# Transposing the feed-forward activations on VectorE and with small DMAs in place of TensorE, in a two-layer decoder trunk

## What is computed

```python
def swiglu(x, w_gate, w_up, w_down):
    return (jax.nn.silu(x @ w_gate) * (x @ w_up)) @ w_down

for layer in range(DEPTH):
    h = h + 0.5 * swiglu(rms_norm(h, ln_ffn1[layer]), ffn1_w_gate[layer], ffn1_w_up[layer], ffn1_w_down[layer])
    u = rms_norm(h, ln_mix[layer])
    ...
    h = h + 0.5 * swiglu(rms_norm(h, ln_ffn2[layer]), ffn2_w_gate[layer], ffn2_w_up[layer], ffn2_w_down[layer])
return rms_norm(h, final_norm)
```

## Time and profile before

| | us |
|---|---|
| median of 3 runs | 977.7 |
| lowest and highest | 976.63, 978.82 |
| span of the profiled execution, first to last instruction | 974.3 |
| TensorE busy | 954.1 |
| VectorE busy | 522.1 |
| ScalarE busy | 456.0 |
| GpSimd busy | 99.3 |

### The profile page before, as it was taken

The page is one execution under the profiler, slowest core; times in us unless marked ns, Lnnn a source line. Parts: engine busy times, 40 slices in busy tenths (PEclk is TensorE's granted clock), DMA queues, the critical chain, the costliest instruction groups (busy, mean ns, idle before and its releaser), DMA issues.

```text
span 974.3 us, 11825 instructions
## 1 busy us (share of the span) xinstructions
PE 954.1 (98%) x4572; PEld 789.0 (81%) x4572; DVE 522.1 (54%) x480; ACT 456.0 (47%) x583; POOL 99.3 (10%) x170
## 2 busy tenths in 40 slices
PE   6999999999999999999999999999998999999997
PEld 5888888888877888888888888888886888888885
DVE  3654454463576655554466555544547465555442
ACT  4554452354676544443344444433456454444431
POOL 3800000025311100000003000000023010000000
PEclk9999999999999999999999999999999999999999
DMA  9866655444522556664564566645544056665421
GB/s 273 275 199 194 215 196 216 173 173 173 194 89 85 173 178 197 198 226 171 177 201 140 186 200 197 246 163 197 192 151 131 3 185 200 196 199 227 152 113 44
DMA packets 121211, 172.92 MB, mean 177 GB/s; under 512 B 5456, under 2 KB 97632, under 8 KB 121168
## 3 DMA queue, kind: packets, MB, share of 16 engines
q1 hardware_dynamic: 120848, 171.99, 51.9%
q0 software_dynamic: 320, 0.34, 0.4%
HBM read 171.25 MB, written 1.05 MB: 177 GB/s over the span
## 4 chain that ended last, share of the span: by engine, by line
PE 92%; DVE 3%; ACT 2%; DMA 1%; SPq 1%; issue 0%; DVEq 0%; POOLq 0%; POOL 0%; ACTq 0%
PE bank L392 57%; PE bank L427 19%; PE bank L431 9%; PE bank L445 4%; DMA raw<-in_ffn_w_up 1%; DVE w_lo L1353 1%; ACT h L1154 1%; DVE mx L1454 1%; PE bank L612 1%; PE bank L547 1%; ACT w_hi L1051 1%; PE bank L570 1%; SPq L775 1%; ACT silu L1154 0%; DVE shared L1479 0%; PE bank L408 0%
## 5 line engine op out<-in xcount | busy, mean ns | idle before, releaser
L1353 DVE TENSOR_TENSOR w_lo<-raw,w_hi 128x2048 fp32r<-128x2048 f32 x152 | 348.6, 2295 | 224.6 <-ACT w_hi L1051 224.6
L1051 ACT ACTIVATE w_hi<-raw 128x2048 fp32r<-128x2048 f32 x152 | 291.7, 1920 | 204.9 <-PE bank L392 115.1
L392 PE MATMUL bank<-w_hi,xT_hi 128*128 128x512 f32 x832 | 331.2, 398 | 5.3 <-DVE w_lo L1535 5.3
L392 PE MATMUL bank<-w_hi,xT_lo 128*128 128x512 f32 x832 | 325.7, 392 | 0.0
L392 PE MATMUL bank<-w_lo,xT_hi 128*128 128x512 f32 x832 | 325.3, 391 | 0.0
L392 PEld LDWEIGHTS bank<-w_hi,xT_hi 128*128 128x128 f32 x832 | 157.0, 189 | 37.6 <-issue 3.6
L392 PEld LDWEIGHTS bank<-w_hi,xT_lo 128*128 128x128 f32 x832 | 156.9, 189 | 33.6
L392 PEld LDWEIGHTS bank<-w_lo,xT_hi 128*128 128x128 f32 x832 | 157.3, 189 | 30.9
L427 PE MATMUL bank<-w_hi,hT_hi 128*128 128x512 f32 x348 | 136.6, 392 | 0.0
L427 PE MATMUL bank<-w_lo,hT_hi 128*128 128x512 f32 x348 | 135.5, 389 | 0.0
L431 PE MATMUL bank<-w_hi,hT_lo 128*128 128x512 f32 x348 | 107.3, 389 | 0.0
(11 more groups left out here) (142 smaller groups left out, 627.3 us busy)
## 6 DMA issues: line engine op xcount, KB each, us to landing
raw<-in_ffn_w_gate SPq DMA_DIRECT2D x88, 512.0 KB, 4.2
raw<-in_ffn_w_up SPq DMA_DIRECT2D x88, 512.0 KB, 5.3
raw<-in_ffn_w_down SPq DMA_DIRECT2D x88, 512.0 KB, 4.2
raw<-in_a_w_qkv SPq DMA_DIRECT2D x24, 512.0 KB, 5.0
raw<-in_a_w_o SPq DMA_DIRECT2D x8, 512.0 KB, 4.0
raw<-in_b_w_q SPq DMA_DIRECT2D x8, 512.0 KB, 4.8
raw<-in_b_w_o SPq DMA_DIRECT2D x8, 512.0 KB, 3.9
vec<-in_ln_ffn SPq DMA_DIRECT2D x4, 512.0 KB, 5.7
```

What stands on the lines that cost most here:

```text
L392: mm = nc.tensor.matmul(bank[b][:, :], xs[:, kt, own(pos)], ws[:, slot(u), cols], start=(kt == 0 and i == 0), stop=(kt == KT - 1 and i == 2))
L1051: nc.scalar.activation(w_parts(u)[0], raw[:, slot(u), :], ACT.Copy).then_inc(s_hi, 1)
L1353: nc.vector.tensor_tensor(lo, raw[:, slot(u), :], hi.bitcast(F32), ALU.subtract).then_inc(s_lo, 1)
```

## The change

The transposes of the five full blocks leave TensorE. VectorE transposes the block of 128x512 in squares of 32x32 into the buffer of `silu` (called `turned`), with the column groups reordered. SyncE then issues 16 DMAs from SBUF to SBUF, each 32 partitions x 128 columns (16 KB), which put square row a, column group q to partition group q, columns of a, in the first 512 columns of `xn` (called `landed`). ScalarE and VectorE read `landed` for hi and lo in place of a PSUM bank. The last 256 columns are still transposed by TensorE. The moves of pos 0 stand in SyncE's queue eight ahead of a unit's load and eight ahead of the next one's; those of pos 1 are together behind a turn's loads. On ScalarE and VectorE the parts of pos 0 move behind silu/mul(1,1), those of pos 1 into the next turn, behind its first two splits, and those of block 4 of pos 1 ahead of silu/mul(1,0) at the end of the stage. The down stage waits for a count of the lo parts in place of PSUM reads. SyncE's `gate_up`, the vectors and the `rows` of a feed-forward are joined in one `ffn`; the order of the loads among themselves stays.

```diff
+        turned = [silu[:, pos, :, :].rearrange("p j n -> p (j n)") for pos in range(NPOS)]
+        landed = [xn[:, pos, 0:BANK] for pos in range(NPOS)]
...
+        def block_no(f, g):
+            return H_BLOCKS * f + g + 1
...
-        FILLED_PER_TURN = 4
+        FILLED_PER_TURN = 2
...
# TensorE
                     gate_up(4 * g, 1, 0, g, turn)
-                    h_transposes(0, (f, g), turn)
                     gate_up(4 * g + 2, 1, 1, g, turn)
                     gate_up(4 * g + 4, 0, 0, g + 1, turn)
-                    h_transposes(1, (f, g), turn)
...
-                h_transposes(0, (f, 5), n_tiles=2)
+                h_transposes(0, f)
...
-                pe.wait_ge(s_read[4], uses[4] - 1)
+                pe.wait_ge(s_hT_lo[0], block_no(f, H_BLOCKS - 1))
                 down((0, 1), 0)
-                h_transposes(1, (f, 5), n_tiles=2)
+                h_transposes(1, f)
                 down((2,), 0)
-                pe.wait_ge(s_read[6], uses[6] - 1)
+                pe.wait_ge(s_hT_lo[1], block_no(f, H_BLOCKS - 1))
...
# SyncE
+            def h_move(f, pos, g, rows):
+                sp.wait_ge(s_turned[pos], block_no(f, g))
+                for a in rows:
+                    for q in range(4):
+                        sp.dma_start(landed[pos][32 * q:32 * (q + 1), P * a:P * (a + 1)],
+                                     turned[pos][32 * a:32 * (a + 1), P * q:P * (q + 1)]).then_inc(s_hT[pos], 16)
...
+                with sp.Fori(0, LOOP_TURNS) as turn:
+                    for k in range(2):
+                        h_move(f, 0, turn, (2 * k, 2 * k + 1))
+                        unit(u0 + 8 + k, k, turn * (2 * CH) + 4 * CH, turn)
+                    for k in range(2):
+                        unit(u0 + 10 + k, k, turn * (2 * CH) + 5 * CH, turn)
+                    h_move(f, 1, turn, range(4))
                 for k in range(2):
+                    h_move(f, 0, 3, (2 * k, 2 * k + 1))
                     unit(u0 + 20 + k, k, CH * (N_CHUNK - 1))
+                for name in vectors:
+                    vector(name)
+                down(0, 1)
+                h_move(f, 1, 3, range(4))
+                for k in range(2):
+                    h_move(f, 0, 4, (2 * k, 2 * k + 1))
+                    down(2 + k)
+                down(4, 5)
+                h_move(f, 1, 4, range(4))
+                down(*range(6, DN_UNITS))
...
# ScalarE
+                def h_hi(pos, g, turn=0):
+                    act.wait_ge(s_hT[pos], (block_no(f, g) + turn) * 16 * H_MOVES)
+                    nc.scalar.activation(hT_hi[:, bass.ds((g + turn) * 4, 4), own(pos)].rearrange("p t (q s) -> p t q s", q=4),
+                                         landed[pos].rearrange("p (q t s) -> p t q s", q=4, t=4),
+                                         ACT.Copy).then_inc(s_hipart, 1)
...
                     split(u0 + 4 * g + 4, turn)
                     split(u0 + 4 * g + 5, turn)
+                    if g:
+                        h_hi(1, g - 1, 0 if turn is None else turn)
                     silu_gate(1, 0, g, turn)
-                    h_hi(0, g, turn)
                     split(u0 + 4 * g + 6, turn)
                     split(u0 + 4 * g + 7, turn)
                     silu_gate(1, 1, g, turn)
+                    h_hi(0, g, 0 if turn is None else turn)
                     silu_gate(0, 0, g + 1, turn)
-                    h_hi(1, g, turn)
...
                 split(u0 + 24)
                 split(u0 + 25)
+                h_hi(1, 4)
                 silu_gate(1, 0, 5)
...
# VectorE
+                def h_turned(pos, g, turn=0):
+                    b, n = taken["gu", f, g, 1, pos]
+                    dve.wait_ge(s_read[b], n + turn)
+                    nc.vector.transpose(turned[pos].rearrange("p (q t s) -> p t q s", q=4, t=4),
+                                        h[:, pos, :].rearrange("p (t q s) -> p t q s", t=4, q=4)
+                                        ).then_inc(s_turned[pos], 1)
...
+                    h_turned(0, g, 0 if turn is None else turn)
                     split(u0 + 4 * g + 4, turn)
                     split(u0 + 4 * g + 5, turn)
+                    if g:
+                        h_lo(1, g - 1, 0 if turn is None else turn)
                     mul(1, 0)
-                    h_lo(0, g, turn)
                     split(u0 + 4 * g + 6, turn)
                     split(u0 + 4 * g + 7, turn)
                     mul(1, 1)
+                    h_turned(1, g, 0 if turn is None else turn)
+                    h_lo(0, g, 0 if turn is None else turn)
                     mul(0, 0)
-                    h_lo(1, g, turn)
```

More of the change, by code:

```diff
@@ L53 @@
 FFN_UNITS = GU_UNITS + DN_UNITS
+H_BLOCKS = N_CHUNK // 2
+H_MOVES = 16
 HEADS = 8
@@ L238, in trunk @@
         s_silu = sem("s_silu")
+        s_turned = [sem(f"s_turned{i}") for i in range(NPOS)]
+        s_hT = [sem(f"s_hT{i}") for i in range(NPOS)]
+        s_hT_lo = [sem(f"s_hT_lo{i}") for i in range(NPOS)]
         s_hipart = sem("s_hipart")
@@ L460, in x_ready, with h_transposes @@
                     in_sbuf(pe, ("xT", name, pos, j))
[L462 to L467, removed]
+            def h_transposes(pos, f):
+                b = acc(pos, 0)
+                pe.wait_ge(s_read[b], uses[b])
+                transposes([h[:, pos, P * i:P * (i + 1)] for i in range(2)], 4 + 2 * pos, ("hT", f, pos))
             def ffn(f, u0, name, next_name):
@@ L785, in unit @@
                              for i, w in enumerate((gate, up))], turn)
-                for k in range(4):
+                for k in range(8):
                     unit(u0 + k, k % 2, CH * (k // 2))
@@ L790, in gate_up, with down @@
                         load_x(1)
-                with sp.Fori(0, 4) as turn:
-                    for k in range(4):
-                        unit(u0 + 4 + k, k % 2, turn * (2 * CH) + CH * (2 + k // 2), turn)
+                def down(*ts):
+                    view = w_down[l].rearrange("(k p) n -> p k n", p=P)
+                    for i in ts:
+                        u = u0 + GU_UNITS + i
+                        dst = raw[:, slot(u), :].rearrange("p (k n) -> p k n", k=2)
+                        load(u, [(dst[:, k, :], view[:, 2 * i + k, :]) for k in range(2)])
+                with sp.Fori(0, LOOP_TURNS) as turn:
[5 more added lines that the diff above has]
+                    h_move(f, 1, turn, range(4))
                 for k in range(2):
+                    h_move(f, 0, 3, (2 * k, 2 * k + 1))
                     unit(u0 + 20 + k, k, CH * (N_CHUNK - 1))
+                for name in vectors:
[8 more added lines that the diff above has]
+                down(*range(6, DN_UNITS))
             def rows(u0, n, w):
@@ L836, in _ @@
             vector("ln_ffn1_0")
[L837 to L841, removed]
+            ffn(0, U_FFN1_0, a["ffn1_w_gate"], a["ffn1_w_up"], a["ffn1_w_down"], 0, "ln_mix_0", "ln_ffn2_0", "kv_norm")
             columns(U_QKV, 6, a["a_w_qkv"][0])
@@ L844, in _ @@
             vector("ln_ffn1_1")
-            gate_up(U_FFN2_0, a["ffn2_w_gate"], a["ffn2_w_up"], 0)
-            vector("ln_mix_1")
-            rows(U_FFN2_0 + GU_UNITS, DN_UNITS, a["ffn2_w_down"][0])
+            ffn(1, U_FFN2_0, a["ffn2_w_gate"], a["ffn2_w_up"], a["ffn2_w_down"], 0, "ln_mix_1")
             dst = raw[:, slot(U_KV), :].rearrange("p (k g c) -> p k g c", k=KT, g=2)
@@ L850, in _ @@
                         for i, w in enumerate(("kv_w_k", "kv_w_v"))])
[L851 to L854, removed]
+            ffn(2, U_FFN1_1, a["ffn1_w_gate"], a["ffn1_w_up"], a["ffn1_w_down"], 1, "b_b_q", "b_b_o")
             columns(U_WQ, 2, a["b_w_q"][0])
@@ L857, in _ @@
             vector("ln_ffn2_1")
-            gate_up(U_FFN2_1, a["ffn2_w_gate"], a["ffn2_w_up"], 1)
-            vector("final_norm")
-            rows(U_FFN2_1 + GU_UNITS, DN_UNITS, a["ffn2_w_down"][1])
+            ffn(3, U_FFN2_1, a["ffn2_w_gate"], a["ffn2_w_up"], a["ffn2_w_down"], 1, "final_norm")
             sp.wait_ge(s_xn, xn_count("final_norm", 0))
@@ L1091, in silu_gate, with h_last_hi @@
                     nc.scalar.activation(silu[:, pos, j, :], bank[acc(pos, j)][:, 0:CH], ACT.Silu).then_inc(s_silu, 1)
[L1093 to L1096, removed]
+                def h_hi(pos, g, turn=0):
[3 more added lines that the diff above has]
+                                         ACT.Copy).then_inc(s_hipart, 1)
+                def h_last_hi(pos):
+                    hi_part(hT_hi[:, FT - 2:FT, own(pos)], 4 + 2 * pos, ("hT", f, pos), 2)
                 def turn_of(g, turn=None):
@@ L1122, in ffn @@
                 split(u0 + 25)
+                h_hi(1, 4)
                 silu_gate(1, 0, 5)
-                h_hi(0, 5, n_tiles=2)
-                h_hi(1, 5, n_tiles=2)
+                h_last_hi(0)
+                h_last_hi(1)
                 for i in range(26, 33):
@@ L1407, in mul, with h_lo, h_last_lo @@
                                             ALU.mult).then_inc(s_read[b], 1)
```

(16 more changed lines are left out.)

2 lines of the change are left out of this document (1 added, 1 removed).

## The result

The change makes the kernel slower: 1063.67 us median (4 runs, 1061.92 to 1064.24) beside 977.96 for the kernel before on the same chip, a ratio of 1.0877 with a 95% interval of 1.0862 to 1.0892. The forecast was 959.3 us. The profiled span is 1062.2 us where it was 974.3. (In every execution that has both on record the time is 1.8 us above the span. So 974.3 stands for some 976.1 us, a little low for the kernel before, and the 3.4 us between its span and its median are partly chance.)

The account below looks back on a forecast made before the run. TensorE, busy 954.1 of 974.3 us, was taken as the bound; removing 40 transpose groups at 0.46 saves 18.4, added work costs zero, giving a 955.9 span plus 3.4, 959.3 us; range 957 to 966.

Parts of the forecast that it names:

- The saving: Gate/up stage on TensorE: 40 groups of four transposes removed at 0.46 us each, 18.4 us off the path.
- added durations: Rival reading of TensorE's transposes: durations add up, 160 x 0.272 = 43.5 us saved, 934.2 us; chance of its rival 0.01.
- VectorE and ScalarE's order: Feed-forward: VectorE's 40 added transposes at 0.69 us fit idle time, ScalarE stays ready for its next silu; cost zero.
- the price of an issue: SyncE's queue: each small move taken at 0.34 us, between almost nothing and 0.77; no stall under 0.48.
- The second term of the same sum: SyncE's queue in a full turn: four load pairs at 0.80 us beside 32 moves, 14.1 us in all.
- The upper end, 0.77: SyncE's queue: highest price assumed for one move, an issue with others outstanding, 0.77 us.
- rival 2: SyncE's queue: moves overfill the turn from 0.58 us each, loads slip, gain gone at 0.61, 1079 us at 0.77; chance 0.08.
- rival 1: End of each feed-forward's gate/up stage: at 0.55 us an issue TensorE stands 1.1 us, four times, 963.7 us; chance 0.10.
- The rings: DMA rings: moves take 4.3 us a turn, 0.20 on a mean share of 0.52, so they fit.
- The count of packets: DMA rings: 16 KB moves of 32 rows of 512 bytes, a block bringing 32 packets to each engine, 2.1 us.

## Why the prediction was wrong

**The saving** was right: 18.4 forecast, 18.5 less busy time of TensorE without the moves, and 958.18 us for that kernel where 959.3 were forecast. The reading of starts, not of durations, was the right one; added durations would have given 43.5.

**VectorE and ScalarE's order** were right, at no cost: 958.18 us without the moves.

**The step that failed** is the price of an issue: "I take 0.34, the lowest of the steady rows, since a transfer of 16 KB should not cost more than one of 512". It costs 0.63 us, with single ones of up to 1.88, so that a row of 24 behind loads averages 0.70 to 0.74. The argument by size was void, as size does not enter; what enters is SBUF on both sides, and no row of before had that. The second term of the same sum was low too: a load unit takes 1.17 us of the queue from its first issue to the next unit's, not 0.80. Together 4 x 0.80 + 32 x 0.34 = 14.1 was in truth 27.3 to 28.1, more than TensorE's 21.8.

**The bounds were stated and the range was not drawn to them.** The upper end, 0.77, held the measured average (though not the single issues: before has some of up to 3.96), and rival 2 had the threshold at 0.58 and the gain gone at 0.61. Between 0.34 and 0.77 the measured value lies past both. With such a threshold in the middle of an unknown's interval, 0.08 was too small a chance, and a range that ended at 966 left it out.

**Rival 2 was the mechanism, and its price was off.** By its formula 0.63 gives 20 x (3.2 + 20.2 - 21.8) = 32 us on 959.3, 991. Measured are 105.7 on 956.5: 66 in the turns, 39 at the ends and in the down stages behind them. The formula's prices were too low (the single slow issues, the loads' own 1.17), but its count of 20 full turns was too high: with the measured turn it gives 20 x (27.3 - 21.8) = 110 us, and the turns lose 66, and only 48 of that waiting, as the first blocks of each feed-forward are moved without a wait to speak of. The end of the stage is rival 1's term, which rival 2 didn't add, and no term had TensorE's clock: 31.7 us of the loss are matmuls at the lower level, 18 in the turns and 13.5 at the ends and in the down stages.

The link was also another than was written. Loads did not slip first; the moved block was late, and ScalarE waited for it in order, with splits and silus behind. ScalarE's longest wait in total, after:

```profile
ACT hT_hi L1125 <- DMA xn<-silu: 237.8, 40, 11.2
```

One such turn, ScalarE and then TensorE in the first feed-forward:

```profile
119.61 0.63 ACT L1125 ACTIVATE hT_hi<-xn 128x512 f32 x1 [7.31 <-DMA xn<-silu]
...
120.41 3.70 ACT L1080 ACTIVATE w_hi<-raw 128x2048 fp32r<-128x2048 f32 x2
```
```profile
124.69 0.50 PE L404 MATMUL bank<-w_hi,xT_hi 128*128 128x512 f32 x1 [3.47 <-DVE w_lo L1389]
```

After 7.31 us of waiting two splits follow without a pause: their data was there. TensorE's stop is for w_lo of the first of these, one link further. In all TensorE waits 27.2 us for w_lo in eight such stops, and 6.2 for h in three.

**Rival 1**, the end of the stage, was right in place and in formula: 16 us per us of issue over 0.48 gives 16 x (0.63 - 0.48) = 2.4 us. Measured are 7.6 to 8.1, because the sixteen moves begin late. In the first feed-forward:

```profile
160.60 10.43 SPq L791 DMA_DIRECT2D xn<-silu  x16
```

They were forecast to begin at 138.7, 5.9 us ahead of the transposes of pos 0 (144.58). They begin 0.1 us behind them (160.50), and in the other three 0.1 to 0.3 behind. These 6 us and the 2.4 make up the loss, less some tenths for a landing of 1.8 to 2.0 instead of 2.1. VectorE turns the block later (1.5 to 4.6 us ahead of those transposes), and the queue takes it up another 1.6 to 4.7 later.

**The rings** were right in what they cost: 52.4% of the span, and bytes and packets cost nothing that a run shows. The count of packets was low: 151568 - 120848 over 640 moves is 48 a move, not 32.

What stays open: why two SBUF sides cost 0.17 us more an issue, and why single issues take up to 1.9 us.

## What to carry to other kernels

Count the issues of each queue in a steady turn and price them by the distance from one issue to the next, on a DMA with the same kinds of memory on both sides; bytes say nothing of this cost, here from 4 KB to 256 KB. When the sum comes near the turn's time, what decides is a threshold, so put the range across it, and remember that an in-order engine which waits for the late transfer holds up everything behind it. Before giving up an idea for its many small DMAs, share them with a queue that is idle: here that turned 8.8% slower into 1.8% faster.

## What the runs showed of the hardware that was not expected

- A DMA issue by SyncE with SBUF on both sides takes 0.63 to 0.65 us of its queue from start to start, for 4 KB as for 16, 64 and 256 KB and for 32 partitions as for 128; with DRAM on one side 0.45 to 0.48, for 16 KB as for a load of 512.
- Behind 3 MB of loads queued in 4 us most of these issues stay at 0.63 us, but single ones take up to 1.9, and the last load before them 1.1 to 1.3: a mean over 24 of 0.70 to 0.74 hides this.
- GpSimd issued the small SBUF-to-SBUF moves faster, at 0.49 us each, with a landing like SyncE's (medians 3.7 and 3.6 us).
- Four float32 transposes of 128x128 cost TensorE's stream 0.46 us in all (18.5 / 40), though each shows 272 ns.
- TensorE's slow matmuls go on behind the wait: the four down stages, without any idle time, take 228.4 us where they take 220.2 without the moves.
